# First attention of a two-block kernel: scores of four heads at a time, and p turned by DMA moves and 32x32 blocks on VectorE in place of TensorE

## What is computed

```python
scores = jnp.einsum('bnqhgd,bnkhd->bnhgqk', q, kb) * (HEAD_DIM ** -0.5)
scores = scores - slopes[:, :, None, None] * dist
scores = jnp.where(valid[None, :, None, None], scores, NEG)
p = jax.nn.softmax(jnp.concatenate([scores, sink_col], axis=-1), axis=-1)[..., :-1]
o = jnp.einsum('bnhgqk,bnkhd->bnqhgd', p, vb).reshape(B, S, BRANCH)
...
y = (o.astype(z.dtype) * jax.nn.silu(z)) @ w_out
```

## Time and profile before

| | us |
|---|---|
| median of 3 runs | 1769.11 (1768.79 to 1769.21) |
| the profiled execution | 1768.36 |
| its span in the trace | 1766.7 |
| TensorE busy | 1755.2 |
| VectorE busy | 1269.5 |
| ScalarE busy | 882.3 |
| GpSimd busy | 204.4 |

### The profile page before, as it was taken

How to read it: one execution, slowest core, us unless ns; L and a number is a source line. 1 busy time by engine, 2 the same in 40 slices (tenths; PEclk the granted TensorE clock), 3 DMA queues, 4 the chain that set the end, 5 groups by cost and what they waited for, 6 DMA issues and landing times.

```text
span 1766.7 us, 24966 instructions
## 1 busy us (share of the span) xinstructions
PE 1755.2 (99%) x8130; PEld 1444.6 (82%) x8130; DVE 1269.5 (72%) x1649; ACT 882.3 (50%) x1235; POOL 204.4 (12%) x377
## 2 busy tenths in 40 slices
PE   9999999999999999999999999999999999999998
PEld 7777778887888888888888888888888888888886
DVE  5787779777988788777678768777775654554455
ACT  6876685545444354444445455444444444444443
POOL 1111101010233332410001101000000000000000
PEclk9999999999999999999999999999999999999999
DMA  9888778655798898898998958999998865555554
GB/s 336 299 299 250 251 260 305 208 163 175 236 272 288 272 302 266 272 317 294 319 315 296 319 169 270 314 314 313 309 298 238 237 215 193 195 193 191 191 194 138
DMA packets 201711, 454.29 MB, mean 257 GB/s; under 512 B 20160, under 2 KB 31408, under 8 KB 201264
## 3 DMA queue, kind: packets, MB, share of 16 engines
q1 hardware_dynamic: 168080, 343.28, 60.0%
q0 software_dynamic: 33424, 110.19, 18.8%
q10 hardware_dynamic: 144, 0.03, 0.0%
HBM read 434.03 MB, written 12.06 MB: 252 GB/s over the span
## 4 chain that ended last, share of the span: by engine, by line
PE 96%; DVE 2%; DMA 1%; ACT 1%; SPq 0%; issue 0%; DVEq 0%; ACTq 0%
PE bank L1684 30%; PE bank L1685 30%; PE bank L1686 30%; DMA raw<-in_w_in_a 1%; PE bank L1850 1%; PE bank L1730 1%; PE bank L1840 1%; DVE w_lo L1070 0%; PE bank L1942 0%; PE bank L1831 0%; PE bank L1955 0%; PE bank L1828 0%; DVE x L1097 0%; PE bank L1710 0%; ACT y L661 0%; DVE y L1676 0%
## 5 line engine op out<-in xcount | busy, mean ns | idle before, releaser
L1070 DVE TENSOR_TENSOR w_lo<-raw,w_hi 128x1024 fp32r<-128x1024 f32 x605 | 731.6, 1214 | 433.1 <-ACT w_hi L657 431.6
L657 ACT ACTIVATE w_hi<-raw 128x1024 fp32r<-128x1024 f32 x605 | 634.3, 1050 | 751.3 <-PE bank L1686 665.5
L1684 PE MATMUL bank<-w_hi,h_hi 128*128 128x512 f32 x2272 | 892.2, 393 | 1.6 <-DVE w_lo L1180 0.5
L1686 PE MATMUL bank<-w_hi,h_lo 128*128 128x512 f32 x2272 | 885.2, 390 | 0.0
L1685 PE MATMUL bank<-w_lo,h_hi 128*128 128x512 f32 x2272 | 885.1, 390 | 0.0
L1684 PEld LDWEIGHTS bank<-w_hi,h_hi 128*128 128x128 f32 x2272 | 426.9, 188 | 95.5 <-issue 4.4
L1686 PEld LDWEIGHTS bank<-w_hi,h_lo 128*128 128x128 f32 x2272 | 426.7, 188 | 89.6
L1685 PEld LDWEIGHTS bank<-w_lo,h_hi 128*128 128x128 f32 x2272 | 427.1, 188 | 86.2
L541 POOL DMA_DIRECT2D ada_raw<-in_w_ada x160 | 85.3, 533 | 749.9 <-DVE acc_a L1077 524.2
L1077 DVE SCALAR_TENSOR_TENSOR acc_a<-ada_raw,cond,acc_a 128x1024 f32<-128x1024 f32 x112 | 143.2, 1279 | 2.8 <-DMA ada_raw<-in_w_ada 2.6
L1077 DVE SCALAR_TENSOR_TENSOR acc_b<-ada_raw,cond,acc_b 128x1024 f32<-128x1024 f32 x48 | 62.4, 1300 | 1.5 <-DMA ada_raw<-in_w_ada 1.5
(11 more groups left out here) (211 smaller groups left out, 930.2 us busy)
## 6 DMA issues: line engine op xcount, KB each, us to landing
raw<-in_w_ff SPq DMA_DIRECT2D x256, 512.0 KB, 4.6
raw<-in_w_in SPq DMA_DIRECT2D x176, 512.0 KB, 5.0
ada_raw<-in_w_ada POOLq DMA_DIRECT2D x160, 512.0 KB, 5.9
raw<-in_w_in_a SPq DMA_DIRECT2D x69, 512.0 KB, 5.3
ada_more<-in_w_ada POOLq DMA_DIRECT2D x32, 512.0 KB, 6.0
raw<-in_w_out_a SPq DMA_DIRECT2D x32, 512.0 KB, 5.9
raw<-in_w_o SPq DMA_DIRECT2D x32, 512.0 KB, 5.0
raw<-in_w_moba SPq DMA_DIRECT2D x16, 512.0 KB, 5.5
```

Of the source, the lines that this page charges most:

```text
L657: act.activation(used(w_hi, turn, s), used(raw, turn, s), ACT.Copy).then_inc(hi_ready, 1)
L1070: dve.tensor_tensor(used(w_lo, turn, s), used(raw, turn, s), used(w_hi, turn, s).bitcast(F32), ALU.subtract).then_inc(lo_ready, 1)
L1684: pe.matmul(out_ap, hi, rhs_hi, start=start, stop=False)
L1686: return pe.matmul(out_ap, lo, rhs_hi, start=False, stop=stop)
```

## The change

Iterations 0 to 2 of the first attention work in two batches of four heads. TensorE scores four heads in one slot (2 and 6) into four banks, and multiplies the values of four heads in one slot (10 and 14). ScalarE's exp writes p to `p_blk` or the new `p1_blk` in blocks of 32 columns instead of in place. GpSimd moves the blocks with 16 DMAs for a batch (`move_heads1`), behind a few loads for ada; VectorE turns them in 32x32 blocks at slots 9 and 13 (`turn_p1`), four heads each, into `p1_t` and two other places that are free then. The six turns of a pair on TensorE and the copies of p on ScalarE are gone in these iterations. The second batch's moves wait until the first batch has been turned, since both pass through `sums_r`. The ada units get other slots and four buffers of lead; GpSimd's loop is unrolled. Iteration 3 keeps the old way and gets semaphores of its own. `rstd_diag` and `rstd_row` now share `norm_rows`. The core of the diff:

```diff
 CHUNK_GATE, CHUNK_YAB, CHUNK_WO, CHUNK_FF1 = 28, 30, 44, 48
 CHUNKS = D // CH
 PAIRS_A = GROUP_A // 2
-STEPS = (2, 4, 6, 8, 10, 12)
+HEADS_BATCH = GROUP_A // 2
+SLOTS_SCORES, SLOTS_BACK, SLOTS_OUT = (2, 6), (9, 13), (10, 14)
 SLOT_SUMS, SLOT_GATE, SLOT_TURN = 10, 12, 14
 STEPS_LAST = (2, 4, 6, 8, 10, 11)
-ADA_ROWS_0, ADA_GAIN_0 = (4, 5, 6, 7), tuple(range(8, 16))
-ADA_ROWS, ADA_GAIN = (0, 1, 2, 4), (6, 8, 9, 10, 11, 13, 14, 15)
+ADA_ROWS_0, ADA_GAIN_0 = (2, 5, 5, 6), (9, 10, 11, 11, 13, 14, 14, 15)
+ADA_ROWS, ADA_GAIN = (0, 1, 1, 2), (5, 5, 6, 10, 11, 11, 14, 14)
 SUMS_LAST, GATE_LAST, TURN_LAST = 11, 11, 12
-ADA_FIRST, ADA_AHEAD = 64, 2
+ADA_FIRST, ADA_AHEAD = 64, 4
 FIRST_BY_K = 3
...
         ones_r = sb("ones_r", [P, P], F32R)
         sums_r = sb("sums_r", [P, 3, CH], F32R)
-        rstd_diag = sb("rstd_diag", [P, T, P])
-        rstd_row = sb("rstd_row", [P, SEQ])
+        norm_rows = sb("norm_rows", [P, CH])
+        rstd_diag = norm_rows[:, 0:T * P].rearrange("p (t n) -> p t n", t=T)
+        rstd_row = norm_rows[:, SEQ:2 * SEQ]
...
+            p1_blk = sb("p1_blk", [P, HEADS_BATCH * MASK_W], on=a)
...
+        p1_blocks = (p_blk, p1_blk[:, :])
+        p1_heads = (p1_t[:, 0, :], p1_t[:, 1, :], post_gain[:, 4 * MASK_W:5 * MASK_W], norm_rows[:, 0:MASK_W])
+        p1_moved = sem("p1_moved")
+        p1_t_last = sem("p1_t_last")
...
-            def load_ahead(i, units):
+            def move_heads1(i, b):
+                pool.wait_ge(p1_ready, i * GROUP_A + (b + 1) * HEADS_BATCH + 2)
+                if i + b:
+                    pool.wait_ge(p1_t_ready, (2 * i + b) * HEADS_BATCH)
+                for q in range(QUADS):
+                    for r in range(QUADS):
+                        move_p(pool, p1_blocks[b], p1_moved, q, r)
+            def load_units(i, units):
                 for n in units:
-                    load_group(i, n + ADA_AHEAD)
+                    load_group(i, n)
...
-            with pool.Fori(0, CHUNKS - 1) as i:
-                load_ahead(i, range(12))
-            load_ahead(CHUNKS - 1, range(4 - ADA_AHEAD))
-            pool.wait_ge(h_lo_ready, H_NORM0 + UPT)
+            for i in range(CHUNKS - 1):
+                load_units(i, range(4, 7) if i == 0 else range(4, 10))
+                move_heads1(i, 0)
+                load_units(i, range(7, 9) if i == 0 else range(10, 11))
+                move_heads1(i, 1)
+                load_units(i, range(9 if i == 0 else 11, 16))
+            pool.wait_ge(o1_ready, (CHUNKS - 1) * PAIRS_A + 2)
             load_gain(0, g_post)
...
+            def attn1_exp_blocks(i, k):
+                act.wait_ge(neg1_ready, i * GROUP_A + k + 1)
+                blocks = p1_blocks[k // HEADS_BATCH].rearrange("p (j h b d) -> p h b j d", j=QUADS, h=HEADS_BATCH, b=3)
+                dst = blocks[:, k % HEADS_BATCH]
+                act.activation(dst[:, 0], s1[:, k % 2, 0:P].rearrange("p (j d) -> p j d", j=QUADS), ACT.Exp,
+                               bias=neg_cur[:, k, 0:1], scale=SCALE_A, accum_out=l_cur[:, k, 0:1])
+                act.activation(dst[:, 1:3], s1[:, k % 2, P:MASK_W].rearrange("p (b j d) -> p b j d", b=2, j=QUADS), ACT.Exp,
+                               bias=neg_cur[:, k, 1:2], scale=SCALE_A, accum_out=l_cur[:, k, 1:2]).then_inc(p1_ready, 1)
+            def keep_batch(i, b):
+                act.wait_ge(o1_ready, i * PAIRS_A + 2 * b + 4)
+                act.activation(o_t[:, 2 * b:2 * b + 2, :], two(banks[SCORES + b][:, :]), ACT.Copy).then_inc(o1_kept, 2)
...
+            def batch_slot(i, n):
+                if n == 0:
+                    for j in range(2):
+                        bias(i, j)
+                if n == 1:
+                    turn_q1(i)
+                for b, at in enumerate(SLOTS_SCORES):
+                    first = b * HEADS_BATCH
+                    if n == at + 1:
+                        for k in range(2):
+                            attn1_exp_blocks(i, first + k)
+                            bias(i, first + k + 2)
+                    if n == at + 2:
+                        for k in range(2, 4):
+                            attn1_exp_blocks(i, first + k)
+                    if n == at + 3 and b == 0:
+                        for k in range(2):
+                            bias(i, HEADS_BATCH + k)
+                if n == SLOT_SUMS:
+                    sink_share(i)
+                    z_sigmoid(i, i * 2 + TURN_ZQ)
+                if n == SLOTS_OUT[0] + 1:
+                    keep_batch(i, 0)
             def attn1_front(i, m):
                 if 1 <= m <= PAIRS_A:
...
-            def attn1_scores(i, j):
+            def attn1_scores(i, j, last=False):
                 h = i * GROUP_A + j
+                scores = banks[SCORES + j % (2 if last else HEADS_BATCH)]
                 dve.wait_ge(bias_ready, h + 1)
                 dve.wait_ge(s1_ready, h + 1)
-                dve.wait_ge(p1_turned, i * PAIRS_A + j // 2 + 1)
+                if last and j >= 2:
+                    dve.wait_ge(p1_turned, j // 2)
+                else:
+                    dve.wait_ge(p1_ready, h + 1)
                 if j == 0:
                     dve.wait_ge(heads_cur, i + 1)
...
+            p1_returned = p_back.rearrange("p (i h b d) -> p h b i d", i=QUADS, h=HEADS_BATCH, b=3)
+            def turn_p1(i, b):
+                dve.wait_ge(p1_moved, i * (2 * MOVES) + (b + 1) * MOVES)
+                dve.wait_ge(o1_ready, i * PAIRS_A + 2 * b + 2)
+                for k in range(HEADS_BATCH):
+                    dve.transpose(p1_heads[k], p1_returned[:, k]).then_inc(p1_t_ready, 1)
+            def batch_slot(i, n):
+                here = [b * HEADS_BATCH + 2 * half for b, at in enumerate(SLOTS_SCORES) for half in range(2) if n == at + 1 + half]
+                for j in here:
+                    attn1_scores(i, j)
+                split(i * 2 + TURN_ZQ + n // UPT, n % UPT + AHEAD)
+                for j in here:
+                    attn1_scores(i, j + 1)
+                if n in SLOTS_BACK:
+                    turn_p1(i, SLOTS_BACK.index(n))
+                if n == SLOT_SUMS:
+                    sums1(i)
+                if n == SLOT_GATE:
+                    gate_o(i)
...
-                        at = rows_at.index(n)
-                        ada_first(i * 12 + 4, at, acc_b, i * 2 + at // 2)
-                    if n in gain_at:
-                        at = gain_at.index(n)
-                        ada_first(i * 12 + 8, at, acc_a, i * 4 + 2 + at // 2)
+                    for at in range(4):
+                        if rows_at[at] == n:
+                            ada_first(i * 12 + 4, at, acc_b, i * 2 + at // 2)
+                    for at in range(8):
+                        if gain_at[at] == n:
+                            ada_first(i * 12 + 8, at, acc_a, i * 4 + 2 + at // 2)
             attn1_turns(0, ADA_ROWS_0, ADA_GAIN_0)
             with dve.Fori(1, CHUNKS - 1) as i:
                 attn1_turns(i, ADA_ROWS, ADA_GAIN)
...
+            def scores1_batch(i, b):
+                if b == 0:
+                    pe.wait_ge(q1_t_ready, i * T + T)
+                    pe.wait_ge(kv_cur_ready, i * 2 + 2)
+                    pe.wait_ge(o1_kept, i * PAIRS_A + 1)
+                pe.wait_ge(s1_masked, i * GROUP_A + b * HEADS_BATCH + 2)
+                lanes = (slice(0, DH_A), slice(DH_A, 2 * DH_A))
+                for m in range(2):
+                    q = q1_t[:, 2 * b + m, :]
+                    for n, lane in enumerate(lanes):
+                        pe.matmul(banks[SCORES + 2 * m + n][:, 0:P], q[lane, 0:P], k1_cur[lane, 0:P], start=True, stop=True)
+                    for n, lane in enumerate(lanes):
+                        pe.matmul(banks[SCORES + 2 * m + n][:, P:MASK_W], q[lane, P:SEQ], k1_cur[lane, :],
+                                  start=True, stop=True).then_inc(s1_ready, 1)
+            def outs1_batch(i, b):
+                pe.wait_ge(p1_t_ready, i * GROUP_A + (b + 1) * HEADS_BATCH)
+                pe.wait_ge(s1_masked, i * GROUP_A + GROUP_A + 2)
+                lanes = (slice(0, DH_A), slice(DH_A, 2 * DH_A))
+                for m in range(2):
+                    out = banks[SCORES + b][:, m * SEQ:(m + 1) * SEQ]
+                    for n, lane in enumerate(lanes):
+                        pe.matmul(out[lane, :], v1_cur[:, 0, :], p1_heads[2 * m + n][:, 0:SEQ], start=True, stop=False)
+                    for n, lane in enumerate(lanes):
+                        ins = pe.matmul(out[lane, P:SEQ], v1_cur[:, 1, :], p1_heads[2 * m + n][:, SEQ:MASK_W],
+                                        start=False, stop=True)
+                    ins.then_inc(o1_ready, 1)
+            def batch_slot(i, n):
+                if n == 1:
+                    turn_q1(i)
+                if n in SLOTS_SCORES:
+                    scores1_batch(i, SLOTS_SCORES.index(n))
+                if n in SLOTS_OUT:
+                    outs1_batch(i, SLOTS_OUT.index(n))
+                if n == SLOT_TURN:
```

(24 more changed lines are left out.)

31 lines of the change are left out of this document (14 added, 17 removed).

## The result

The changed kernel takes 1789.65 us, median of 4 runs (1788.01 to 1792.02). The kernel before, on the same chip, takes 1768.95 (1767.55 to 1769.21). The ratio is 1.0119, 95% interval 1.0107 to 1.0131: 20.7 us slower. The forecast was 1787.2 with a range of 1765 to 1802. In the profiled execution the span is 1786.5 us, 19.8 more than before; that execution took 1788.23 us, 1.4 less than the median.

The account below looks back on a forecast made before the run. TensorE, busy 99% of the span, was taken as the bound. Span 1766.7 plus 18.1 us lost in three passes gives 1784.8, with 1.7 around it 1786.5, and 0.75 for the median: 1787.2 us, range 1765 to 1802.

Parts of the forecast that it names:

- The sum: Iterations 0 to 2: TensorE's waits outweigh the work it is spared, losing 7.3, 5.4 and 5.4 us, together 18.1.
- The chain to the first values: Scores to slot 10's values: batch 0 turned at 34.6 us after unit 2, wanted at 28.5, so TensorE waits 6.
- My 13.0: Microseconds from first issue of a batch's 16 moves to its turns, chosen between 9.6 and 15.6.
- The second set: Batch 1 for slot 14: issued from 34.8, landed 47.8, turned 49.8 us after unit 2; TensorE waits 2.4.
- the fallback: With the fastest moves, VectorE's own order ends batch 1's turns at 49.6; 4 to 5 us lost all the same.
- TensorE is spared: Fewer turns and bursts on TensorE: 3.0 to 4.3 us less work a pass, taken as 3.0.
- load 8: Iteration 0: this load on GpSimd stands before the second moves and waits for an ada unit, 2.4 us more.
- Rival 3: TensorE's clock falls in the new gaps, costing 2.7 us behind each of slot 14: 8 us, 1795; chance 0.10.
- sign of being wrong: One of the listed signs: the clock row shows less than 1.00 and a loss beyond the gaps.
- Rival 1: Turned p comes in time for both batches, leaving only the saving of 9 to 13 us: 1756 to 1760; chance 0.12.
- Rival 4: The change doesn't do what it says: 72 of 96 turns would still be on TensorE; under 1 in 100.
- Rival 2: Moves as slow as in the second attention, 15.6 instead of 13.0 us: 15.6 more in all, 1803; chance 0.13.

Follow-up runs that it names:

- e9: e8 with VectorE's two gain ada units of slot 11 and one more moved behind the second turns: 1765.58 us, ratio 0.9984 to the kernel before.
- e5: Changed kernel with ScalarE's copies w_hi for slots 4, 5, 8, 9 and 11 issued one step earlier: 1780.48 us, ratio 1.0067 to the kernel before.
- e1: Changed kernel without the 16 transfers of p behind each batch, counted as landed at once: 1783.74 us, ratio 1.0083 to the kernel before.
- e8: e6 with a second landing buffer, so batch 1's moves needn't wait for batch 0's turns: 1762.59 us, ratio 0.9964 to the kernel before.
- e2: Changed kernel with gain ada units in later slots (iterations 1 and 2) and batch 0's moves issued earlier: 1783.99 us, ratio 1.0082 to the kernel before.
- e3: Changed kernel with 20 filling products of 128x128 ahead of TensorE's wait in slot 10: 1792.03 us, ratio 1.0135 to the kernel before.
- e6: Changed kernel with the changes of e2 and e5 together: 1764.41 us, ratio 0.9979 to the kernel before.
- e7: Changed kernel without p's transfers and without VectorE's turns of the first attention in iterations 0 to 2: 1768.61 us, ratio 1.0002 to the kernel before.

## Why the prediction was right, step by step

**The sum.** I had 18.1 us in three passes (7.3, 5.4, 5.4). Measured are 5.6, 5.5 and 7.3, together 18.4. Unit 2 of iteration 0 also started 0.67 us later than before; since over the other runs it started anywhere from 58.38 to 60.09 (59.43 before), that is not of the change. 18.4 + 0.7 is 19.1 of the span's 19.8. That the sum is so near is partly luck: iteration 0 was charged 1.7 us too much and iteration 2 1.9 too little. The median lay 1.4 us above the profiled execution where I had added 0.75.

**The chain to the first values**, point by point in iteration 1, predicted and measured: head 0 at 5.2 and 5.3; the ada units of slot 5 end at 18.4 and 18.3; moves at 19.6 and 19.1; first issue to turns 13.0 and 13.1; turns end at 34.6 and 34.2; TensorE wants them at 28.5 and 28.2; wait 6 and 6.07. The row that carried most was the earlier trace rows, the turns behind the same moves elsewhere in the kernel: bounds of 9.6 and 15.6, and in all runs together, where VectorE waited for batch 0, it was 11.9 (e9, iteration 2) to 15.1 (e5, iteration 0). My 13.0 was a choice between the bounds; in the kernel after it was 12.5, 13.1 and 14.4.

**The second set.** I had the moves landed at 47.8, and VectorE's own order as the fallback, with turns that end at 49.6. It was the fallback: VectorE came at 48.0, waited for no DMA, and ended at 49.9. The two bounds lay so near each other that the sum didn't feel which one held, and that is luck too: the term that the sum names, the moves landing at 47.8, is not what ended the wait. e1 and e5 brought this out: I had charged the moves, but taking them away alone returns 6 us, and removing only ScalarE's delay of VectorE returns 9. The gaps of 1.56, 2.00 and 2.61 us were in my chain (split 7 ends at 12.7 behind ScalarE) but I had treated them as given.

**Terms that were off.** TensorE is spared more: e8's passes less their waits are 43.08, 43.08 and 43.16, so a pass of TensorE's work is 43.1 against 46.8, 3.7 us and not 3.0. So in iteration 1 the loss of 5.5 is made up of waits of 6.9 (I had 8.4), 2.3 of slow clock (I had 0) and 3.7 spared (I had 3.0); the three come out right together because the end of VectorE's second turns sets the pass, whatever TensorE does before. A batch of four scores costs 1.51 rather than 1.72, as the second pair follows without a gap of its own, and four heads' values cost 1.45 at full clock rather than 1.6. Iteration 0 was charged 2.4 us for load 8, which stood in front of the second moves. They started at 35.1, 2.0 us behind the first turns, against 34.7 and 0.6 in iteration 1, but those turns had come a microsecond earlier; and slot 14 was bound by VectorE in any case. Iteration 2 was under-charged: its moves took 14.4 us to the turns, and the second 16 are broken by a pause of 2.34 us in GpSimd's issue that ends in no wait.

**The rivals.** Rival 3 named what happened: the clock fell to 0.50 behind each gap of slot 10. Its price, 2.7 us behind each gap of slot 14, didn't come. TensorE lost 2.9, 2.3 and 1.8 us behind slot 10 (pass, less waits, less 43.1), hidden under slot 14's wait, and behind slot 14 it didn't fall. I had called it a sign of being wrong if the clock is down and there is a loss beyond the gaps; the clock was down, and the loss beyond them was taken up. In e1, e2, e3 and e6, where that wait was 2.37 us or more, it fell there too; then the values take up to 2.76 us instead of 1.45, and that stands in the time. The Trainium skill, "TensorE: Matmul & The Clock Gate", Part 1, knows just these two levels and the fall after idle time; the rows agree. Rival 1, all in time, is what e8 approaches: 1762.6. My condition for it was less than 9 us between slot 5's ada unit and the turns. It came from another side, that of taking those units out of the chain (e2) together with ScalarE's order (e5), which I had not weighed. Rival 4 is out: 24 of TensorE's 96 turns of p are left (L1960), those of iteration 3. Rival 2, the slow moves, came in part, in iteration 2 and in e5.

**The rule of the Trainium skill** ("VectorE: DVE Perf Modes", "Rules for kernel authors") to turn 128x128 on TensorE held for the kernel as changed, but not for e8: with 24 turns more on VectorE and 96 small transfers in place of 72 turns on TensorE the kernel is 6 us faster, once hardly anything waits for them (1.1 to 1.7 us a pass).

## What to carry to other kernels

When work leaves the engine that sets the time, write down for each engine on the new route when it arrives at its step by its own order, beside when the data arrive: here the two lay 1.04 us apart in the pass that is shown. Taking the transfers out alone gave back 6 us of 21, taking the engine's stalls out alone (e5) 9, starting the transfers earlier alone (e2) 6, and e2 and e5 together 25. Short stalls between two engines that are busy 49% and 72% of the span cost nothing until the bound engine waits for their chain; here they were the largest single thing to remove, by issuing five copies one step earlier. Work put off in one pass of a loop can come back in the next: in e7 and e9 VectorE came 2 us late to a pass because of the one before. Filling a gap to keep a clock up gave nothing where a later wait on the same route took up the difference (e3, iteration 0).
